# Moving half of the value projection, the bonus sums and the gate projection into the waits of the inversion, in an RWKV-7 and attention trunk

## What is computed

```python
def rwkv7_time_mix(x, ...):
    h = rms_norm(x, norm_g); dx = shift(h) - h
    xr, xw, xk, xv, xa, xg = (h + dx * mu[i] for i in range(6))
    r, k, v = xr @ w_r, xk @ w_k, xv @ w_v
    w = -softplus(-(w0 + tanh(xw @ w1) @ w2)) - 0.5
    a = sigmoid(a0 + (xa @ a1) @ a2)
    g = sigmoid(xg @ g1) @ g2
    kk = normalised(k * k_k); k = k * (1 + (a - 1) * k_a)
    o = wkv7_scan(r, exp(-exp(w)), k, v, -kk, kk * a)   # delta rule, 16 heads of 64
    o = group_norm(o) * lnx_g + lnx_b
    bonus = sum(r * k * r_k, per head) * v
    return ((o + bonus) * g) @ w_o
```

## Time and profile before

| | us |
|---|---|
| median of 3 runs | 1041.26 |
| the three runs | 1044.86, 1038.76, 1041.26 |
| the profiled execution | 1039.32 |
| its span from first to last instruction | 1037.5 |
| mean granted TensorE clock | 0.971 of full speed |
| TensorE busy with matmuls | 977.0 |
| VectorE busy | 686.4 |
| ScalarE busy | 424.4 |

### The profile page before, as it was taken

The page is one execution under the profiler, slowest core; times in us unless marked ns, Lnnn a source line. Parts: engine busy times, 40 slices in busy tenths (PEclk is TensorE's granted clock), DMA queues, the critical chain, the costliest instruction groups (busy, mean ns, idle before and its releaser), DMA issues.

```text
span 1037.5 us, 17071 instructions
## 1 busy us (share of the span) xinstructions
PE 977.0 (94%) x6488; PEld 825.9 (80%) x6488; DVE 686.4 (66%) x1287; ACT 424.4 (41%) x661; POOL 72.7 (7%) x54
## 2 busy tenths in 40 slices
PE   5989989989887999999968999999999979999998
PEld 4768668678674888888868999999999558888887
DVE  6774783755756476666568887887787336666664
ACT  3301303114112544444344665666555426444442
POOL 0100000000000000000002211221212000000000
PEclk9989999999977999999989999999999989999999
DMA  9310040310510666666449545455454135766661
GB/s 305 110 53 2 18 158 1 123 53 1 163 42 0 178 187 182 184 188 193 145 117 296 161 142 143 129 146 153 123 152 134 42 100 147 217 183 182 182 184 59
DMA packets 194835, 136.88 MB, mean 132 GB/s; under 512 B 7246, under 2 KB 185934, under 8 KB 194652
## 3 DMA queue, kind: packets, MB, share of 16 engines
q1 hardware_dynamic: 194780, 136.10, 45.2%
HBM read 135.03 MB, written 1.05 MB: 131 GB/s over the span
## 4 chain that ended last, share of the span: by engine, by line
PE 81%; DVE 8%; issue 7%; ACT 1%; DMA 1%; POOL 1%; SPq 0%; POOLq 0%; ACTq 0%
PE bank L408 46%; PE wide L408 32%; DVE work L1103 3%; DVE work L1312 1%; PE wide L778 1%; DVE x L1103 1%; DVE work L1321 1%; POOL gsm L1555 1%; PE bank L778 0%; DVE wsp L1103 0%; DMA x<-in_x 0%; PE bank L758 0%; PE wide L758 0%; DMA ring<-in_w_kv 0%; PE bank L431 0%
## 5 line engine op out<-in xcount | busy, mean ns | idle before, releaser
L408 PE MATMUL bank<-wpj,hkq 128*128 128x384 f32 x1152 | 215.3, 340 | 1.4 <-ACT once L845 1.2
L408 PEld LDWEIGHTS bank<-wpj,hkq 128*128 128x128 f32 x1152 | 198.7, 189 | 6.6 <-issue 5.2
L408 PE MATMUL wide<-hsp,wsp 128*128 128x512 f32 (+1 forms) x1056 | 197.7, 345 | 3.1 <-DVE hsp L1103 3.1
L408 PEld LDWEIGHTS wide<-hsp,wsp 128*128 128x128 f32 x1056 | 168.5, 193 | 29.9 <-DVE hsp L1103 3.6
L1103 DVE TENSOR_TENSOR wsp<-ring,wsp 128x1024 fp32r<-128x1024 f32 (+1 forms) x88 | 150.7, 1752 | 3.5 <-ACT wsp L845 3.5
L845 ACT ACTIVATE wsp<-ring 128x1024 fp32r<-128x1024 f32 (+1 forms) x88 | 130.5, 1484 | 19.8 <-PE wide L408 14.0
L408 PE MATMUL bank<-work 64*64 64x64 f32 (+5 forms) x1200 | 78.9, 248 | 22.9 <-DVE work L1312 14.8
L408 PE MATMUL bank<-wsp,asp 128*128 128x512 f32 x396 | 98.1, 392 | 0.0
L1555 POOL TENSOR_TENSOR gsm<-gsm,mhalf 128x6 f32<-128x6 f32 (+1 forms) x40 | 63.5, 1653 | 490.3 <-DVE gsm L1235 273.7
L1103 DVE TENSOR_TENSOR wpj<-ring,wpj 128x1536 fp32r<-128x1536 f32 x48 | 84.2, 1754 | 17.8 <-ACT wpj L845 17.7
L408 PEld LDWEIGHTS bank<-work 64*64 64x64 f32 (+3 forms) x1200 | 63.1, 149 | 38.7 <-DVE work L1312 20.6
(11 more groups left out here) (171 smaller groups left out, 1093.8 us busy)
## 6 DMA issues: line engine op xcount, KB each, us to landing
ring<-in_f_w_gu SPq DMA_DIRECT2D x88, 512.0 KB, 5.9
ring<-in_w_kv SPq DMA_DIRECT2D x96, 256.0 KB, 3.5
ring<-in_f_w_down SPq DMA_DIRECT2D x44, 512.0 KB, 3.8
ring<-in_b_w_q SPq DMA_DIRECT2D x48, 256.0 KB, 3.5
wmix<-in_a_w_k SPq DMA_DIRECT2D x4, 1024.0 KB, 7.5
wmix<-in_a_w_r SPq DMA_DIRECT2D x4, 1024.0 KB, 10.1
wmix<-in_a_w_v SPq DMA_DIRECT2D x4, 1024.0 KB, 6.1
wmix<-in_a_w_o SPq DMA_DIRECT2D x4, 1024.0 KB, 5.2
```

What stands on the lines that cost most here:

```text
L408: return pe.matmul(o, a, b, start=start, stop=stop)
```

## The change

The gate projection leaves its place before the values. EARLY goes from 3 to 2: in groups 1 to 3 two quarters of the value projection are left, and both run in round 1 between X of q = 0 and X of q = 1. The bonus sums run after round 1, the gate projection's two halves after rounds 2 and 3. TensorE waits for `act_g` after the inversion, ScalarE copies the gate after the keys and the values.

```diff
-        EARLY = 3
+        EARLY = 2
@@ TensorE
                 mm(bank[3], halves, sq...).then_inc(S("pe_ss"), 1)
-                for n in range(2):
-                    mm(bank[5][:, n * T:(n + 1) * T], g2s[:, 0, n * P:(n + 1) * P], tg[:, 0, :], True, False)
-                    m = mm(bank[5][:, n * T:(n + 1) * T], g2s[0:LG - P, 1, n * P:(n + 1) * P], tg[0:LG - P, 1, :], False, True)
-                m.then_inc(S("pe_g"), 1)
@@
                 project(6, 2, xv, "pe_v", [early - 1])
                 if behind:
                     pe.wait_ge(S("dve_xadd"), it * 4)
-                pe.wait_ge(S("dve_rkr"), it + 1)
-                mm(bank[7], halves, rkr.rearrange("p n t -> p (n t)")).then_inc(S("pe_bonus"), 1)
-
                 pe.wait_ge(S("dve_scaled"), it + 1)
...
-                pe.wait_ge(S("act_g"), it + 1)
@@
                 def values_fill(l):
-                    if l + early < 4:
-                        project(6, 2, xv, "pe_v", [l + early])
+                    if l == 0:
+                        project(6, 2, xv, "pe_v", range(early, 4))
+                    elif l == 1:
+                        pe.wait_ge(S("dve_rkr"), it + 1)
+                        mm(bank[7], halves, rkr.rearrange("p n t -> p (n t)")).then_inc(S("pe_bonus"), 1)
+                    elif l in (2, 3):
+                        n = l - 2
+                        mm(bank[5][...], g2s[:, 0, ...], tg[:, 0, :], True, False)
+                        m = mm(bank[5][...], g2s[0:LG - P, 1, ...], tg[0:LG - P, 1, :], False, True)
+                        if n == 1:
+                            m.then_inc(S("pe_g"), 1)
@@
-                values_fill(0)
                 pe.wait_ge(S("act_kn"), it + 1)
                 for l in range(1, LEVELS - 1):
                     for q in range(2):
...
                         m.then_inc(S("pe_X"), 1)
+                        if l == 1 and q == 0:
+                            values_fill(0)
@@ after the rounds
+                pe.wait_ge(S("act_g"), it + 1)
@@ ScalarE: the wait on pe_g, the wait on dve_y and the copy
                 A(gT, bank[5], ACT.Copy).then_inc(S("act_g"), 1)
   go from before the copies of kPn and bPn to behind the copy of vT
```

More of the change, by code:

```diff
@@ L543, in values_fill @@
                 def values_fill(l):
-                    if l + early < 4:
-                        project(6, 2, xv, "pe_v", [l + early])
+                    if l == 0:
[5 more added lines that the diff above has]
+                        n = l - 2
+                        mm(bank[5][:, n * T:(n + 1) * T], g2s[:, 0, n * P:(n + 1) * P], tg[:, 0, :], True, False)
+                        m = mm(bank[5][:, n * T:(n + 1) * T], g2s[0:LG - P, 1, n * P:(n + 1) * P], tg[0:LG - P, 1, :], False, True)
+                        if n == 1:
+                            m.then_inc(S("pe_g"), 1)
                     elif l == 4:
@@ L909, in group @@
                 A(nrm, rn, ACT.Sqrt).then_inc(S("act_nrm"), 1)
[L910 to L913, removed]
                 act.wait_ge(S("pe_tk"), it + 1)
@@ L923, in group @@
                     A(wsp[:, 1, 0, 2048:3072], raw[0][:, 2048:3072], ACT.Copy).then_inc(S("act_dn_hi"), 1)
+                act.wait_ge(S("pe_g"), it + 1)
+                if behind:
+                    act.wait_ge(S("dve_y"), it)
+                A(gT, bank[5], ACT.Copy).then_inc(S("act_g"), 1)
                 act.wait_ge(S("pe_tv"), it + 1)
```

## The result

| | before | changed |
|---|---|---|
| median, us | 1041.9 (8 runs) | 1036.56 (8 runs) |
| lowest and highest run | 1038.76, 1045.35 | 1033.78, 1039.86 |
| profiled execution, span | 1037.5 | 1035.3 |
| mean granted clock | 0.971 | 0.975 |

The ratio of the changed kernel to the one before is 0.9947, with a 95% interval from 0.9929 to 0.9964. Measured a second time it was 0.9970 (0.9956 to 0.9984), with a median of 1037.53 against 1040.36. The two intervals just overlap; what they have in common is a gain of 0.36 to 0.44%, some 4 us of 1040.

What follows compares the result with a forecast made beforehand. In a group the bound was taken to change from TensorE's list to VectorE, then rounds handing work between both, then TensorE. Gains 3 x 0.47 + 0.39 = 1.80 off the median 1041.26 gave 1039.5; range 1033.5 to 1047.5.

Steps and rivals of the forecast that it cites:

- (a): Rival: the fills go into TensorE's waits altogether, only the head counts, 8.5 us less, 1032.8; chance 0.13.
- The head of groups 1 to 3: TensorE's list gets 5.03 shorter, but VectorE's additions to x come next, so the head gains only 2.20.
- The long fill: Two value quarters in round 1, 3.70 long; VectorE's second four copies cover all but 0.21: +0.21.
- The rounds: Fills behind rounds 1 to 3 (bonus sums, two gate halves) cost +1.52 together, with the -0.57 behind round 3 included.
- the first fill: Bonus sums behind round 1, 1.17 long, cost 0.81; the second and third fills cost 0.64 each.
- the multiplication for the bonus: VectorE's 0.65 behind round 3 held back round 4's mask by 0.57 and does so no longer: -0.57.
- The sum of a group: For each of groups 1 to 3: -2.20 + 0.21 + 1.52 = -0.47.
- Group 0: No addition is waited for, four quarters stay in the head; head -1.91, with the fills a gain of 0.39.
- The moved copies and transfers: ScalarE's gate copy (0.6) in rounds 3 and 4 and SyncE's later small weights cost nothing; 20 us of cover remain.
- The rule on tile shapes: Tiling changes drain TensorE; two such steps on top of each fill, 0.66 each, 7.9 in all, would give 1047.4.
- (b): Rival: fills cost their whole length, or the head doesn't move; 6.7 more, 1048.0; chance 0.10 in both forms.
- (c): Rival: the clock falls behind the head's new idle stretch, up to 4.6 a group; 1048.7 or more; chance 0.11.

Runs made afterwards that it cites:

- the cut wait: Changed kernel with the wait on `dve_xadd` cut into the waits the banks need (second, third, fourth addition): 1034.83, ratio 0.9937 against the kernel before.
- the last variant: Changed kernel with w_o product banks reordered to 1, 2, 0, 7, the addition wait cut accordingly, bonus sums ahead of round 1: 1030.21, again 1029.74.
- the doubled fills: Changed kernel with each half of the gate projection computed twice in its place behind rounds 2 and 3: 1049.13, ratio 1.0090 against the kernel before.

## Why the prediction was right, point by point

The forecast was 1039.5, the time 1036.56: inside the range and on the side that was forecast. The sum gave a gain of 1.80; the edits as the traces show them are worth 3.4, and the medians differ by 5.3 in the first measurement and 2.8 in the second. Of the 2.9 between forecast and time, 1.6 is the sum's error, worked out below, and the other 1.3 no edit explains. The range helped: it was 14 us wide, and its lower end, 1033.5, is not "halfway to (a)", which would be 1036.1, but nearly at (a). The time is inside by that narrower bound too, by less than 0.5.

*The head of groups 1 to 3.* 2.20 was forecast, 2.36 came. The step that mattered, that the list is 5.03 shorter but VectorE's additions come next, is shown by the releaser of the wait (2.67, by VectorE's addition to x) and by the cut wait, which shortened the head by 1.18 more. The missing 0.16 is the estimate of 0.2 between a load and its first matmul: behind this wait both start at 127.22.

*The long fill.* +0.21 was forecast, 0 came. The term that failed is the 0.33 for the step to the 128-wide tile. The loads of X end at 134.10 and those of the fill begin at 134.17, 0.07 behind them. The 0.33 of the earlier trace rows stands behind matmuls of 256 columns, those of the products and those of the value quarter; X has matmuls of 64 columns. The gap goes by what stands in front of the step (see the tile shapes below), and the row in front of the long fill was the wrong one to take it from.

*The rounds.* +1.52 was forecast. In group 1 the stretch from the first masked copy to the transposes behind round 5 went from 23.91 (130.90 to 154.81) to 154.35 - 128.98 = 25.37, +1.46; the covered value quarters have no part in it. The pattern was as said, with VectorE waiting 0.72 for X. The first X of rounds 4 and 5 in the kernel before:

```profile
147.79 1.47 PE L408 MATMUL bank<-work 64*64 64x64 f32 x32 [0.27 <-DVE work L1312]
...
151.17 1.94 PE L408 MATMUL bank<-work 64*64 64x64 f32 x48
```

From X of the second half in round 1 to the first X of round 2 it was 2.15 and is 2.88, so the first fill cost 0.73 (0.81 forecast). The next two distances were 2.94 and 2.95 and are 3.54, so 0.60 and 0.59 (0.64 each). From round 4 to 5 it was 3.38 and is 2.90: -0.48 (-0.57), the multiplication for the bonus that holds nothing back any more. With the gate halves taken out the rounds were 0.76 shorter, with both doubled 2.5 longer.

*The sum of a group.* -0.47 was forecast, -0.91 to -0.94 came; the difference is made of 0.16, 0.21 and 0.06. All three errors had one sign. Two are small against their terms and the third, the long fill's 0.21, is the whole of its term. Since the sum is a difference of terms of about 2, they doubled it. Only the range covered this; the sum by itself was not better than to a factor of two.

*Group 0.* Its head gained 2.04 (1.91 forecast); its rounds had a lower clock for a part of the time in both traces, as in all twelve, so its sum, 0.67 against 0.39, is not clean.

*The moved copies and transfers.* ScalarE's copy of the gate ran at 147.91 beside round 4 and nobody waited for it. SyncE's last small transfer went out at 149.73 (151 was forecast) and is used more than 20 us later.

*The rule on tile shapes.* The Trainium skill, "TensorEngine Tiling (Array Packing)", section "Key Properties", says that a change of tiling mode drains TensorE. The traces agree: at a change the next loads start the later, the longer the matmuls in front of it are. It is 0.07 behind matmuls of 64 columns (142.94 to 143.01 in the changed kernel), 0.17 behind 128 columns (127.80), 0.33 behind 256 (143.64, 144.26) and 0.76 behind 512 (130.88 in the last variant). The 0.66 a fill that I weighed did not come on top: from the end of U's loads at 142.94 to the loads of the next X at 144.26 it is 1.32 in all, against the 1.24 of the sum.

*The rivals.* (a), fills for nothing, would be 8.5 us in place of 3.4; the doubled fills rule it out. (b), fills at full price or a head that stays, is ruled out by the same stretches. (c) does happen, in two of nine heads, but its price was mis-sized: 1.25 and 1.41, not up to 4.6, because the clock was back before the long fill began. It lengthened the way to the first masked copy; behind that copy VectorE's copies covered it, and the stretch to the end of the rounds was as long as in the other groups (25.38 against 25.36, and 27.89 against 27.88).

*What stays open.* The measured ratios of the changed kernel, 0.9947 and 0.9970, differ by more than 2 us, and the stretches without an edit vary by as much between traces: the part behind group 3's rounds took 740.57 to 744.49 in the twelve traces. In every one of them the granted clock is 0.50 for 17 to 24 us soon behind that point, more than all falls inside the groups together, and TensorE is busy there. The kernel before and the changed one (length, PE, PEld, DVE, ACT, POOL, clock, DMA, GB/s):

```profile
299.00:319.50 20.50, 19.51 (x78) 17.01 (x79) 5.83 (x17) 3.58 (x7) 1.66 (x2) 0.50 0.17 49
```

```profile
296.90:314.00 17.10, 16.24 (x68) 14.85 (x69) 5.24 (x15) 1.69 (x5) 1.01 (x1) 0.50 0.15 40
```

Nothing was tried on this stretch, and what brings the low clock there stays open. Three groups without a fall in round 1 in place of 4 in 9 would be worth some 1.3 us, two falls in nine heads some 0.9 against it; neither number is firm. Which part of the first measurement's extra gain is chance stays open; 3.4 is what the edits show.

## What to carry to other kernels

When work is taken out of one engine's list, ask first which wait stays behind it in the list: here 5.0 us a group were taken out and 2.4 gained. Another 1.2 us a group lay in cutting that wait into the ones that the buffers really need, and 1.8 with the buffers also coming free in the order in which they are needed. An idle time in a loop of two engines that hand work to each other is hardly room: the three fills here, of about 1.2 each, cost 0.73, 0.60 and 0.59, and what was put in beyond them cost its whole length, while a wait covered by one long piece of the other engine's work takes fills for nothing up to its length. When a sum is the small difference of large terms, its error is that of the terms.

## What the runs showed of the hardware

When the tile shape changes, the gap between the end of one group of loads and the start of the next goes by the columns of the matmuls in front, not by the direction. In the traces' first 300 us, at the full clock and with nothing else to wait for, it is 0.07 behind 64 columns, 0.17 behind 128, 0.33 behind 256 and 0.76 behind 512; with no change of shape, between loads of 128x128, it is 0.03 behind 256 columns and 0.24 behind 512. From 128x128 to 64x64 tiles it is 0.07, 0.33 or 0.76 by this alone; from 64x64 to 128x128, behind 64 columns, 0.07; between 128x128 and 32x128, behind 256 columns, 0.33 both ways. Two steps of narrow tiles don't fit as well: 128x32 to 128x64 and 128x64 to 128x128 have 0.41 and 0.38 behind 256.

An idle time of 1.7 to 2.7 us on TensorE is followed by the half clock in some groups and not in others of the same trace. Where it came in a head it cost 1.25 to 1.4 us, in round 1 0.74 to 1.56. One fell on key quarters and products behind the rounds for 1.67, where TensorE had been busy for 0.91 to 1.00 of each of the four microseconds before.
